# The eight modulation slots of the first norm in places of their own, and a ring of two that begins with the query weights

## The chip, the cores and the metric

The kernel runs on one core of one Trainium2 chip. The metric is the device time of one execution in microseconds (us); the time given for a kernel is the median of its runs. Lower is better. Each core has a matrix engine (TensorE, PE in the tables, with its weight loads as PEld), a vector engine (DVE), a scalar engine (ACT), a fourth compute engine (GpSimd, POOL), a sequencer that only issues transfers (SyncE, SP), and 16 DMA engines that carry all transfers, whichever engine issued them.

## The reference, cut to what matters

A two-layer transformer block (x has 512 tokens, a context 256 tokens, width 1024) is followed by a second block with convolution, a recurrence and 32 routed experts. What the change touches is the very start: the modulation vectors and the first norm.

```python
silu_c = jax.nn.silu(c)
silu_cc = jax.nn.silu(c_ctx)
for l in range(DEPTH):
    mod = silu_c @ w_mod[l] + b_mod[l]          # w_mod[l]: 1024 x 6144
    mod_c = silu_cc @ w_mod[l] + b_mod[l]
    sh1, sc1, g1, sh2, sc2, g2 = jnp.split(mod[:, None, :], 6, axis=-1)
    csh1, csc1, cg1, csh2, csc2, cg2 = jnp.split(mod_c, 6)
    h = modulate(rms_norm(x, norm1[l]), sh1, sc1)
    hc = modulate(rms_norm(ctx, norm1[l]), csh1, csc1)
    na_q, na_k, na_v, gq, gk, gv, ga, gb = jnp.split(h @ w_in[l], IN_SPLITS, axis=-1)
    ...
```

The first norm needs `sh1`, `sc1` and their context twins: the first 2048 columns of `w_mod[0]`, which is 8 slots of 256 columns.

## The kernel before, in words

Activations are kept transposed: X is 8 tiles of 128 features by 768 tokens (512 of x, 256 of the context), all of it resident in on-chip memory. All weights of the two layers pass as one stream of slots. A slot is 1024 rows by 256 columns in float32, 128 partitions by 8 KB, 1 MB. They land in `ring`, which has two places: slot n goes to place n % 2. The order of the stream is that of `layer_slots`: for the first layer `mod_head` (8), then `gq` (2, the query weights), `gkv` (1) and so on.

What sets the order around the change is each engine's own program, written out by hand with semaphores:

- **SP** issues every slot (`load`, L464, and `load_at`, L488). Slot n waits until slot n - 2 has been used: for a modulation slot, until TensorE has multiplied with it (`steps`), for any other until GpSimd has made its lower part (`lo_done`).
- **ACT** first issues 18 transfers: `vecs` and `consts` (L1018, L1019), then 8 tiles of x and 8 of the context in turn (L1021, L1022). Then it computes the silu of both condition vectors into `sc2` (L1025), and the squares of the 8 tiles of X (L1046). The first square waits until all 16 tiles of X have landed. Then it makes the upper parts of the two halves of the first query slot (`upper`, L1077) and the root of the mean square (L1050).
- **TensorE** multiplies `sc2` with each modulation slot (L581), waits until DVE has copied the result into `mrow` (L1656), and turns it (`mod_turn`, L570). After the eighth it enters `spread_sum(0)`: it waits for all squares and sums, sums over partitions (L591, L592) and spreads the inverse root (L598). The projections are the products of L553.
- **GpSimd** adds up the squares (`sum_squares`, L1428 and L1431), then makes the lower parts of the first query slot (`lower`, L1440).
- **DVE** copies the modulation rows (L1656), adds the bias (L1635), takes the reciprocal (L1592, L1595), and multiplies X by the scale and the inverse root (L1623).

A product of two float32 matrices is made of three products of upper and lower parts (L553), so a slot has to be split before it can be used. The modulation slots are used as they are (`DIRECT`).

Of the kernel before, what the change touches and what calls it, by code (L numbers as in the profile page):

```python
# [8 lines left out]
KD = D // P  # L9
# [11 lines left out]
RING = 2  # L21
SLOT = KD * 256
# [3 lines left out]

def layer_slots(l):

    first = [("mod_head", 8)] if l == 0 else []
    return first + [("gq", 2), ("gkv", 1), ("nak", 2), ("naq", 2), ("nav", 2),  # L30
                    ("mod_rest", 24 if l == 0 else 16),
                    ("merge", 16), ("w_o", 4), ("ffn_in0", KH), ("ffn_out0", 8), ("ffn_in1", KH), ("ffn_out1", 8)]

# [1 line left out]

WIDTHS = {"merge": (8, 4), "ffn_out0": FFQ, "ffn_out1": FFQ}

EVACUATION = {"mod_head": "-", "mod_rest": "-", "merge": "AAVVAAVV", "w_o": "V", "ffn_in0": "AV", "ffn_in1": "AV",
              "ffn_out0": "--VV", "ffn_out1": "--VV", "w_in2": "AVAVAVAVAAAAAAAA", "w_out2": "V"}

DIRECT = ("mod_head", "mod_rest")

SLOT0 = {}
CHUNKS = []
# [101 lines left out]
NR = NG4 + NE  # L146


def build(nc, stream, vecs, consts, xT, ctxT, bias, experts, router, router_b, lru_w, w_ple, pT, w_gate, out):
    fp32 = mybir.dt.float32  # L150
    f32r = mybir.dt.float32r
    ALU = mybir.AluOpType
# [5 lines left out]
    with es:  # L158
# [3 lines left out]
        def sem(name):  # L162
            return es.enter_context(nc.semaphore(name))
# [3 lines left out]
        def at(name, first, size, dtype=fp32):  # L167


            with ExitStack() as place:  # L170
                if first:
                    place.enter_context(nc.sbuf_tensor(f"below_{name}", [P, first], fp32))
                return place.enter_context(nc.sbuf_tensor(name, [P, size], dtype))

        B0 = 16384
        ring = at("ring", 0, RING * SLOT).rearrange("p (r n) -> p r n", n=SLOT)
        h_parts = at("h_parts", 4096, 2 * KD * T, f32r)
        B = at("first_block", B0, 26112)
        BR = at("half_slots", B0 + 22016, 4 * D, f32r)
        y_parts = at("y_parts", B0 + 9216, 2 * KD * T, f32r)  # L180
# [18 lines left out]
        sc2 = sb("sc2", [P, KD, 32])  # L199
# [25 lines left out]
        V = view(B, 9984, 6, 640)  # L225
# [20 lines left out]
        ps = [es.enter_context(nc.psum_tensor(f"ps{i}", [P, 1024], fp32)) for i in range(4)]  # L246
# [13 lines left out]

        loaded = [sem(f"slot{r}_loaded") for r in range(RING)]
        steps = sem("steps_done")
        evac = {"A": sem("scalar_evacuated"), "V": sem("vector_evacuated")}
        inputs = sem("inputs_loaded")
        x_loaded = sem("x_loaded")
# [161 lines left out]
        def updating_step(n, m):  # L427
# [2 lines left out]
                return 2 * SLOT0[n // 2, "w_o"] + m  # L430
            return 2 * SLOT0[n // 2 - 1, "ffn_out1"] + 4 * (m // 2) + 2 + m % 2

        def raw_half(s):

            n = s // 2
            w = ring[:, n % RING, 0:CHUNKS[n] * 256].rearrange("p (k n) -> p k n", n=256)
            return w[:, :, (s % 2) * P:(s % 2 + 1) * P]
# [14 lines left out]
        @block.sync  # L452
        def _(sp):
            def load(n, i=0):

                m = n - RING
                if m >= 0 and SPLIT[2 * m]:

                    sp.wait_ge(lo_done, 8 * i + splits(2 * m + 1))
                elif m >= 0:  # L460

                    sp.wait_ge(steps, 8 * i + (2 * m + 2))
                k = CHUNKS[n]
                sp.dma_start(ring[:, n % RING, 0:k * 256],  # L464
                             stream[ds(4 * i + n, 1), :, 0:k * 256].rearrange("a p n -> p (a n)"))\
                  .then_inc(loaded[n % RING], 16)

            def load_phase(n0, count):
                for n in range(n0, n0 + min(count, 4)):
                    load(n)  # L470
                rounds = count // 4 - 1
                if rounds > 0:

                    with sp.Fori(1, 1 + rounds) as i:
                        for n in range(n0, n0 + 4):
                            load_at(n, i)
                for n in range(n0 + 4 + 4 * max(rounds, 0), n0 + count):
                    load(n)

            def load_at(n, i):  # L480

                m = n + 4 - RING
                if SPLIT[2 * m]:
                    sp.wait_ge(lo_done, 8 * i + (splits(2 * m + 1) - 8))
                else:
                    sp.wait_ge(steps, 8 * i + (2 * m - 6))
                k = CHUNKS[n]
                sp.dma_start(ring[:, n % RING, 0:k * 256],  # L488
                             stream[ds(4 * i + n, 1), :, 0:k * 256].rearrange("a p n -> p (a n)"))\
                  .then_inc(loaded[n % RING], 16)  # L490

            for l in range(LAYERS):
                for name, count in layer_slots(l):
                    load_phase(SLOT0[l, name], count)
            load_phase(SLOT0[2, "w_in2"], 8)
            load_phase(SLOT0[2, "w_out2"], 4)

            sp.wait_ge(steps, 2 * N_STREAM)
            for q in range(12):
                sp.dma_start(MR[:, q, :], experts[0, q]).then_inc(m_load[q], 16)  # L500
            sp.dma_start(scr[:, 5120:7168], w_ple).then_inc(p_in, 16)
            sp.dma_start(scr[:, 7168:8192], pT).then_inc(p_in, 16)
            sp.wait_ge(r_ok, 1)
            total = sp.value_load(total_i[0:1, 0:1], min_val=PAIRS, max_val=PAIRS * (NL // CAP))
            with sp.Fori(1, total) as i:
                j = i % PAIRS
                for q in range(12):

                    sp.wait_ge(m_steps, 12 * i + (q // 2 * 2 - 10))
                    sp.dma_start(MR[:, q, :], experts[ds(j, 1), q].rearrange("a p n -> p (a n)")).then_inc(m_load[q], 16)  # L510

            sp.wait_ge(m_steps, 12 * total)
            for q in range(4):
                sp.dma_start(MR[:, q, :], w_gate[q]).then_inc(pg_in, 16)

            for k in range(KD):
                sp.wait_ge(x_upd, 17 + k)
                sp.dma_start(out[k * P:(k + 1) * P, :], X[:, k, 0:NL]).then_inc(xo, 16)
            sp.wait_ge(xo, 16 * KD)
# [3 lines left out]
        def _(pe):  # L523
# [38 lines left out]
            kept = []  # L562

            def mod_turn():
# [5 lines left out]
                    last = nc.tensor.matmul(ps[3][:, c:c + 2], mrow[:, half * P:(half + 1) * P], fold, start=True, stop=True)  # L570
                last.then_inc(mod_turned, 1)

            def mod_slot(n, tile, l, first=False):

                if not first:
                    mod_turn()
                wait_slot(n)
                w = ring[:, n % RING, :].rearrange("p (k n) -> p k n", n=256)
                for k in range(KD):
                    g = 32 * (k % 4)  # L580
                    last = nc.tensor.matmul(ps[3][g:g + 32, 512:768], sc2[:, k, :], w[:, k, :], start=k < 4, stop=k >= 4)  # L581
                last.then_inc(steps, 2)
                kept.append((tile, l))

            def spread_sum(n, nt):
# [14 lines left out]

            pe.wait_ge(inputs, 32)
            pe.wait_ge(silu_done, 1)
            for n in range(8):
                mod_slot(n, 2 * n, 0, n == 0)
            mod_turn()

            for l in range(LAYERS):
# [41 lines left out]
                nav = 2 * SLOT0[l, "nav"]  # L649
                for j in range(18):  # L650
                    s = s0 + j
# [179 lines left out]
            for j in range(16):  # L831
                s = s0 + j
# [15 lines left out]
            for j in range(8):  # L848
                t, g = j // 2, j % 2
# [11 lines left out]
            for t in range(4):  # L861
                last = nc.tensor.matmul(ps[2][:, 0:NL], onesm, CV[:, t, :], start=t == 0, stop=t == 3)
# [8 lines left out]
            for j in range(8):  # L871
                s = s0 + j
# [144 lines left out]
        def _(act):  # L1017
# [52 lines left out]
            def upper(s, per=0, i=0):  # L1070

                if not is_split(s):
                    return
                act.wait_ge(loaded[(s // 2) % RING], 4 * per * i + 16 * (s // 4 + 1))

                act.wait_ge(steps, per * i + (s - 1))
                act.activation(part(0, s), raw_half(s), ACT.Copy).then_inc(hi_done, 1)  # L1077

            act.wait_ge(small_ok, 1)
# [508 lines left out]
        def _(dve):  # L1588
# [62 lines left out]
            for l in range(LAYERS):  # L1651
                nc.vector.tensor_scalar(qg8[:, l:l + 1], vcol(f"q_gain{l}"), QSCALE, None, ALU.mult).then_inc(small_q, 1)

            for n in range(8):
                dve.wait_ge(steps, 2 * n + 2)
                nc.vector.tensor_copy(mrow[:, :], ps[3][:, 512:768]).then_inc(mod_kept, 1)  # L1656
            dve.wait_ge(mod_turned, 8)
            mod_add(0, 0, 16)
# [454 lines left out]
def slots(w):  # L2113

    k, n = w.shape
    return w.reshape(k // P, P, n // 256, 256).transpose(2, 1, 0, 3).reshape(n // 256, P, -1)


def lay_out(x):
# [4 lines left out]
    def put(l, name, blocks):  # L2124
        n = SLOT0[l, name]
        for b in blocks:
            z[n:n + b.shape[0], :, :b.shape[2]] = b
            n += b.shape[0]

    for l in range(LAYERS):  # L2130
        wm, w = x["w_mod"][l], x["w_in"][l]
        if l == 0:
            put(0, "mod_head", [slots(wm[:, :2048])])
            put(0, "mod_rest", [slots(wm[:, 2048:]), slots(x["w_mod"][1][:, :2048])])
        else:
            put(1, "mod_rest", [slots(wm[:, 2048:])])
# [56 lines left out]
    def by_rows(a):  # L2193

        return a.reshape(-1, P, a.shape[-1]).transpose(1, 0, 2).reshape(P, -1)

    return {"stream": z, "vecs": v, "consts": constants(), "xT": np.ascontiguousarray(x["x"][0].T[:, BLOCKS]),
            "ctxT": np.ascontiguousarray(x["ctx"][0].T), "bias": bias_tables(x["na_rpb"]), "experts": experts,
            "router": router, "router_b": router_b, "lru_w": np.concatenate([x["lru_w_r_2"], x["lru_w_i_2"]]),
            "w_ple": by_rows(x["w_ple_2"][0]), "pT": by_rows(x["p_2"][0, 0].T[:, BLOCKS]), "w_gate": slots(x["w_ple_gate_2"][0])}  # L2200
# [52 lines left out]
```

## Time and profile before

| what | us |
|---|---|
| median of 3 runs | 3204.75 |
| lowest and highest run | 3204.34, 3209.13 |
| the profiled execution, device time | 3203.88 |
| its span, first to last instruction | 3202.1 |
| PE busy | 2970.2 |
| DVE busy | 958.7 |
| ACT busy | 877.6 |
| POOL busy | 930.2 |

The times of the trace are counted from the first instruction of the span. Busy times are of instructions only; a PE that is busy need not run at its peak, since matmuls are pipelined. In the time slices of the page the matrix engine is busy 60% of the first slice of 80 us and 90% or more of most others. The mean granted TensorE clock is 0.965 of full speed.

### The profile page before, as it was taken

What the parts mean: (1) busy time and instruction counts of PE and PEld (TensorE: products, weight loads), DVE (VectorE), ACT (ScalarE), POOL (GpSimd) and SP (SyncE); (2) the same over time, 40 slices, a digit from 0 to 9 for tenths busy, and PEclk for the clock granted to TensorE, in tenths of its full rate; (3) what the DMA queues carried; (4) which work ended last, traced back from release to release, by engine and by line L of the source; (5) the groups of instructions that cost most, each with busy time, mean ns of one, the idle gap of its engine ahead of it and who ended that gap; (6) DMA issues with size and microseconds to landing.
All of it is one profiled execution on the core that took longest, in us unless ns stands there. A gap on an engine that the chain in (4) does not pass through costs nothing.

```text
span 3202.1 us, 42037 instructions
## 1 busy us (share of the span) xinstructions
PE 2970.2 (93%) x17158; PEld 2241.0 (70%) x17158; DVE 958.7 (30%) x1378; ACT 877.6 (27%) x1415; POOL 930.2 (29%) x707
## 2 busy tenths in 40 slices
PE   6999889998999999899889999998877899999998
PEld 4887678887888888687667778886745645454453
DVE  2505541022110211423531232121494322223224
ACT  3226441123221222325442232223333111111121
POOL 3323223333223223432224444445572000000011
PEclk9999999999999999899999999998988799999999
DMA  5124321111112111123222222322211688888840
GB/s 198 63 72 169 108 67 64 67 53 53 66 49 76 66 51 61 62 80 117 98 67 85 87 85 91 106 84 94 68 43 60 288 327 359 358 358 328 357 166 27
DMA packets 62184, 406.49 MB, mean 127 GB/s; under 512 B 7232, under 2 KB 8656, under 8 KB 18160
## 3 DMA queue, kind: packets, MB, share of 16 engines
q1 hardware_dynamic: 57600, 393.77, 33.0%
q0 software_dynamic: 1872, 6.72, 0.6%
q10 hardware_dynamic: 2592, 4.30, 0.4%
q8 instruction: 88, 1.44, 0.2%
q14 instruction: 32, 0.26, 0.0%
HBM read 402.66 MB, written 2.10 MB: 126 GB/s over the span
## 4 chain that ended last, share of the span: by engine, by line
PE 78%; issue 8%; DVE 7%; POOL 3%; ACT 2%; ACTq 0%; DMA 0%; POOLq 0%; DVEq 0%
PE ps L553 45%; PE ps L942 7%; PE ps L917 4%; PE ps L965 4%; PE ps L712 3%; POOL half_slots L1440 3%; PE ps L739 3%; PE ps L693 2%; DVE second_block L1912 2%; PE ps L1010 2%; PE ps L982 2%; PE ps L581 2%; DVE X L2085 1%; PE ps L570 1%; PE ps L598 1%
## 5 line engine op out<-in xcount | busy, mean ns | idle before, releaser
L553 PE MATMUL ps<-h_parts,half_slots 128*128 128x512 f32 (+1 forms) x6240 | 1233.1, 359 | 44.7 <-POOL half_slots L1440 14.5
L553 PEld LDWEIGHTS ps<-h_parts,half_slots 128*128 128x128 f32 x6240 | 1039.7, 191 | 239.7 <-issue 38.3
L1440 POOL TENSOR_TENSOR half_slots<-ring,half_slots 128x1024 fp32r<-128x1024 f32 (+3 forms) x292 | 631.4, 2163 | 961.2 <-ACT half_slots L1077 960.9
L1077 ACT ACTIVATE half_slots<-ring 128x1024 fp32r<-128x1024 f32 (+3 forms) x292 | 280.3, 961 | 1340.8 <-PE ps L553 1330.0
L553 PE MATMUL ps<-hidden_parts,half_slots 128*128 128x512 f32 (+1 forms) x1584 | 305.1, 355 | 0.0
L553 PEld LDWEIGHTS ps<-hidden_parts,half_slots 128*128 128x128 f32 x1584 | 261.0, 188 | 43.6
L553 PE MATMUL ps<-y_parts,half_slots 128*128 128x512 f32 (+1 forms) x1152 | 230.5, 361 | 9.9 <-DVE y_parts L1766 9.7
L553 PEld LDWEIGHTS ps<-y_parts,half_slots 128*128 128x128 f32 x1152 | 193.9, 192 | 44.5 <-issue 11.7
L942 PE MATMUL ps<-second_block,scratch 128*64 128x512 f32 x1024 | 223.3, 593 | 1.2 <-DVE scratch L2056 0.6
L1428 POOL COPY second_block<-second_block 128x512 f32<-128x512 f32 x4 | 2.5, 628 | 700.6 <-ACT second_block L1046 700.6
L942 PEld LDWEIGHTS ps<-second_block,scratch 128*64 128x64 f32 x1024 | 86.5, 137 | 130.6 <-issue 130.6
L1819 DVE TENSOR_TENSOR first_block<-ps,first_block 128x768 f32<-128x768 f32 (+1 forms) x44 | 36.3, 824 | 434.0 <-PE ps L553 434.0
L1187 ACT ACTIVATE first_block<-ps,small 128x512 f32<-128x512 f32 (+2 forms) x160 | 115.7, 728 | 141.3 <-DVE small L1731 81.7
L1800 DVE SCALAR_TENSOR_TENSOR X<-ps,mod,X 128x512 f32<-128x512 f32 x72 | 45.4, 659 | 357.6 <-PE ps L553 357.6
L712 PE MATMUL ps<-cst,first_block 128*128 128x128 f32 x704 | 106.9, 282 | 32.6 <-ACT first_block L1175 32.6
L917 PEld LDWEIGHTS ps<-scratch,second_block 128*128 128x128 f32 x816 | 103.5, 194 | 30.6 <-issue 26.0
L965 PE MATMUL ps<-second_block,scratch 128*64 128x512 f32 x512 | 113.4, 595 | 11.8 <-ACT scratch L1389 11.8
L917 PE MATMUL ps<-scratch,second_block 128*128 128x128 f32 x816 | 118.3, 282 | 4.5 <-DVE scratch L2060 4.5
L712 PEld LDWEIGHTS ps<-cst,first_block 128*128 128x128 f32 x704 | 74.3, 141 | 64.6 <-ACT first_block L1187 39.5
L1711 DVE COPY first_block<-ps 128x512 f32<-128x512 f32 x112 | 77.3, 690 | 134.8 <-PE ps L712 134.4
L1783 DVE TENSOR_TENSOR first_block<-ps,first_block 128x768 f32<-128x768 f32 (+3 forms) x32 | 26.4, 824 | 295.0 <-PE ps L553 295.0
L1826 DVE TENSOR_TENSOR hidden_parts<-first_block,hidden_parts 128x768 f32 (+3 forms) x44 | 97.3, 2211 | 47.6 <-ACT hidden_parts L1274 47.6
(265 smaller groups left out, 2907.3 us busy)
## 6 DMA issues: line engine op xcount, KB each, us to landing
second_block<-experts SPq DMA_DIRECT2D x192, 1024.0 KB, 8.0
ring<-stream SPq DMA_DIRECT2D x146, 1024.0 KB, 4.9
ring<-stream SPq DMA_DIRECT2D x16, 768.0 KB, 4.2
ring<-stream SPq DMA_DIRECT2D x16, 640.0 KB, 3.9
ring<-stream SPq DMA_DIRECT2D x16, 512.0 KB, 3.6
first_block<-bias POOLq DMA_DIRECT2D x16, 384.0 KB, 4.4
second_block<-w_gate SPq DMA_DIRECT2D x4, 1024.0 KB, 8.0
X<-xT ACTq DMA_DIRECT2D x8, 256.0 KB, 9.2
```

Source lines behind the costliest of these rows:

```text
L553: last = nc.tensor.matmul(ps[s % 2][:, a:b], part(x, s)[:, k, :], parts[y][:, tile + k, a:b], start=start and k == 0 and n == 0, stop=stop ...
L581: last = nc.tensor.matmul(ps[3][g:g + 32, 512:768], sc2[:, k, :], w[:, k, :], start=k < 4, stop=k >= 4)
L712: last = nc.tensor.transpose(ps[2][:, at:at + P], rows[:, (c % nch) * P:(c % nch + 1) * P], ident)
L739: nc.tensor.matmul(ps[3][half * HD:(half + 1) * HD, at:at + P], vals, p_turned(g)[:, (half * nch + c) * P:(half * nch + c + 1) * P], start ...
L917: last = nc.tensor.matmul(ps[0][:, k * P:(k + 1) * P], htok(c, k), SEL[:, c * P:(c + 1) * P], start=c == 0, stop=c == 3)
L942: last = nc.tensor.matmul(ps[1][CAP * x:CAP * x + CAP, 512 * w13:512 * w13 + 512], XG[:, 4 * kk + k, x * CAP:(x + 1) * CAP], w, start=kk = ...
L965: last = nc.tensor.matmul(ps[2][CAP * x:CAP * x + CAP, 512 * n:512 * n + 512], GT[:, 2 * kk + k, x * CAP:(x + 1) * CAP], w, start=kk == 0 ...
L1077: act.activation(part(0, s), raw_half(s), ACT.Copy).then_inc(hi_done, 1)
L1187: act.activation(p_rows(u)[:, 0:width(pairs[i])], ps[half][:, score_cols(g)], ACT.Exp, bias=small[:, 0, u % 8:u % 8 + 1], scale=-1.0 if ki ...
L1440: nc.gpsimd.tensor_tensor(part(1, s), raw_half(s), part(0, s).bitcast(fp32), ALU.subtract)\
L1711: nc.vector.tensor_copy(p_turned(g0 + i)[:, 512 * n:512 * n + 512], ps[2][:, 512 * (j % 2):512 * (j % 2) + 512]).then_inc(s_pt["V"], 1)
L1826: nc.vector.tensor_tensor(dst, g, hi.bitcast(fp32), ALU.subtract).then_inc(gs_lo, 1)
```

## The change

The eight slots of `mod_head` leave the stream and become an input of their own, `mod_head`. Each has its own place in memory, six right behind the ring in what later holds `h_parts`, two in the space of the first block, and a semaphore of its own. SP issues all eight at its start, without a wait. Behind them it issues the first two slots of `gq`, which now are slots 0 and 1 of the ring and have no wait either. TensorE waits for slot n's own semaphore; DVE waits for a new semaphore, `head_steps`. ACT's upper parts of the very first slot no longer wait for `steps`. The stream of the ring is 8 slots shorter, an even number, so every later slot keeps its place.

```diff
-    first = [("mod_head", 8)] if l == 0 else []
-    return first + [("gq", 2), ("gkv", 1), ("nak", 2), ("naq", 2), ("nav", 2),
+    return [("gq", 2), ("gkv", 1), ("nak", 2), ("naq", 2), ("nav", 2),
...
+        head_low, head_high = at("mod_head_low", 4096, 6 * SLOT), at("mod_head_high", B0 + 9216, 2 * SLOT)
...
+        head_in = [sem(f"mod_head{n}_loaded") for n in range(HEAD_SLOTS)]
+        head_steps = sem("mod_head_done")
...
+        def head_slot(n):
+
+            place, at = (head_low, n) if n < 6 else (head_high, n - 6)
+            return place[:, at * SLOT:(at + 1) * SLOT]
...
+            for n in range(HEAD_SLOTS):
+                sp.dma_start(head_slot(n), mod_head[n]).then_inc(head_in[n], 16)
             for l in range(LAYERS):
                 for name, count in layer_slots(l):
                     load_phase(SLOT0[l, name], count)
...
-            for n in range(8):
-                mod_slot(n, 2 * n, 0, n == 0)
+            for n in range(HEAD_SLOTS):
+                if n:
+                    mod_turn()
+                pe.wait_ge(head_in[n], 16)
+                mod_rows(head_slot(n)).then_inc(head_steps, 1)
+                kept.append((2 * n, 0))
             mod_turn()
...
-                act.wait_ge(steps, per * i + (s - 1))
+                if s >= 2:
+                    act.wait_ge(steps, per * i + (s - 1))
...
-            for n in range(8):
-                dve.wait_ge(steps, 2 * n + 2)
+            for n in range(HEAD_SLOTS):
+                dve.wait_ge(head_steps, n + 1)
```

`mod_rows` is the loop of eight matmuls that stood in `mod_slot`, now used by both.

On SP, at the start of the program, before the change (L464 and L488 are the ring's loads, 128x2048 is one slot of 1 MB):

```order
L452 UNCONDITIONAL_BRANCH [waits barrier_Pool_Activation_PE_DVE_SP_release]
L464 DMA ring<-stream 128x2048 x2
L464 DMA ring<-stream 128x2048 [waits steps_done] x2
L474 UNCONDITIONAL_BRANCH
L488 DMA ring<-stream 128x2048 [waits steps_done] x4
L474 REGISTER_ALU
L474 COMPARE_AND_BRANCH
L464 DMA ring<-stream 128x2048 [waits steps_done] x2
L464 DMA ring<-stream 128x2048 [waits both_parts_ready] x9
```

And now (L501 are the eight loads of their own, L472 the ring's):

```order
L460 UNCONDITIONAL_BRANCH [waits barrier_Pool_Activation_PE_DVE_SP_release]
L501 DMA mod_head_low<-mod_head 128x2048 x6
L501 DMA mod_head_high<-mod_head 128x2048 x2
L472 DMA ring<-stream 128x2048 x2
L472 DMA ring<-stream 128x2048 [waits both_parts_ready] x9
```

Two loads without a wait became ten; the first that waits is the third of the ring, for the split of its predecessor.

On TensorE, the end of the head and the start of the norm before (L581 multiplies with a slot, L570 turns its row, L591 begins the sum over partitions):

```order
L581 MATMUL ps<-ring,sc 32x256 [waits slot1_loaded]
L581 MATMUL ps<-ring,sc 32x256 x7
L570 MATMUL ps<-cst,mod_rows 128x2 [waits mod_rows_kept]
L570 MATMUL ps<-cst,mod_rows 128x2
L591 MATMUL ps<-cst,first_block 128x1 [waits squared,squares_summed]
```

And now, at the same place:

```order
L588 MATMUL ps<-mod_head_high,sc 32x256 [waits mod_head7_loaded]
L588 MATMUL ps<-mod_head_high,sc 32x256 x7
L580 MATMUL ps<-cst,mod_rows 128x2 [waits mod_rows_kept]
L580 MATMUL ps<-cst,mod_rows 128x2
L605 MATMUL ps<-cst,first_block 128x1 [waits squared,squares_summed]
```

TensorE's instructions stand in the same order; only what each slot's first matmul waits for is another semaphore. The wait for the squares and their sums stays where it was.

## Rows read from the trace of the kernel before

**Rows 1.** The page: busy time, and the chain that ended last, by engine.

```profile
PE 2970.2 (93%) x17158; PEld 2241.0 (70%) x17158; DVE 958.7 (30%) x1378; ACT 877.6 (27%) x1415; POOL 930.2 (29%) x707
PE 78%; issue 8%; DVE 7%; POOL 3%; ACT 2%; ACTq 0%; DMA 0%; POOLq 0%; DVEq 0%
```

**Rows 2.** Chain in order of time, 0:110 us: start, duration, what.

```profile
15.99 6.11 DMA ring<-stream
...
30.98 5.26 DMA ring<-stream
...
43.20 0.43 PE ps L591 x2
```

**Rows 3.** Timeline: start, duration, engine, line, count, idle before and releaser.

```profile
12.39 1.28 ACT L1025 ACT_TABLE_LOAD   x1 [12.39 <-issue]
...
14.00 1.94 PE L581 MATMUL ps<-ring,sc 128*32 128x256 f32 x16 [14.00 <-ACT sc L1025]
...
25.57 1.93 PE L581 MATMUL ps<-ring,sc 128*32 128x256 f32 x16
...
28.99 1.93 PE L581 MATMUL ps<-ring,sc 128*32 128x256 f32 x16
...
39.71 1.93 PE L581 MATMUL ps<-ring,sc 128*32 128x256 f32 x16
...
43.07 0.56 PE L591 MATMUL ps<-cst,first_block 128*128 128x1 f32 x2
```

**Rows 4.** Waits, 0:60 us, PE: who waited for whom, us in total, times, longest.

```profile
PE ps L581 <- DMA ring<-stream: 1.5, 2, 1.2
```

**Rows 5.** Timeline: the squares and their sum.

```profile
19.70 1.57 ACT L1046 ACTIVATE first_block<-X 128x768 f32<-128x768 f32 x2 [5.79 <-DMA X<-ctxT]
...
21.58 11.58 POOL L1431 TENSOR_TENSOR first_block<-first_block 128x768 f32<-128x768 f32 x6 [0.15 <-POOL first_block L1428]
```

**Rows 6.** DMA view of 3:6 us, then of 6:10 us: queue, packets, MB, share.

```profile
q1 hardware_dynamic: 136, 0.99, 78.4%
q10 hardware_dynamic: 142, 0.25, 21.8%
...
q1 hardware_dynamic: 112, 0.91, 53.6%
q10 hardware_dynamic: 108, 0.81, 48.0%
```

**Rows 7.** Stretches: window, length, PE, PEld, DVE, ACT, POOL busy, PEclk, DMA share, GB/s.

```profile
3.00:6.00 3.00, 0.00 (x0) 0.00 (x0) 0.00 (x0) 0.00 (x0) 0.00 (x0) 1.00 1.00 415
6.00:10.00 4.00, 0.00 (x0) 0.00 (x0) 0.00 (x0) 0.00 (x0) 0.00 (x0) 1.00 1.02 430
11.00:17.00 6.00, 2.46 (x19) 1.21 (x19) 0.64 (x3) 1.50 (x2) 0.00 (x0) 1.00 1.07 377
2472.00:2506.00 34.00, 24.15 (x117) 22.18 (x118) 14.00 (x40) 5.52 (x10) 0.00 (x0) 0.60 1.01 412
```

**Rows 8.** The page, DMA issues: count, KB each, median us to landing.

```profile
X<-xT ACTq DMA_DIRECT2D x8, 256.0 KB, 9.2
X<-ctxT ACTq DMA_DIRECT2D x8, 128.0 KB, 8.9
cst<-consts ACTq DMA_DIRECT2D x1, 947.0 KB, 10.2
vec<-vecs ACTq DMA_DIRECT2D x1, 182.0 KB, 5.8
```

**Rows 9.** Timeline: transfers issued by ACT at the start, by SP before the experts.

```profile
5.47 1.79 ACTq L1022 DMA_DIRECT2D X<-ctxT  x1
...
11.85 0.45 ACTq L1022 DMA_DIRECT2D X<-ctxT  x1
...
2471.18 7.38 SPq L500 DMA_DIRECT2D second_block<-experts  x12
2478.60 2.11 SPq L501 DMA_DIRECT2D scratch<-w_ple  x1
```

**Rows 10.** Timeline: the first query slot's parts, two spreads of equal shape, first product.

```profile
42.99 2.00 ACT L1077 ACTIVATE half_slots<-ring 128x1024 fp32r<-128x1024 f32 x2 [10.84 <-DMA ring<-stream]
...
44.12 4.66 POOL L1440 TENSOR_TENSOR half_slots<-ring,half_slots 128x1024 fp32r<-128x1024 f32 x2 [10.96 <-ACT half_slots L1077]
...
49.90 2.93 PE L598 MATMUL ps<-first_block,cst 128*128 128x512 f32 x4 [1.57 <-DVE first_block L1595]
...
56.49 2.26 PE L553 MATMUL ps<-h_parts,half_slots 128*128 128x512 f32 x6 [3.66 <-DVE h_parts L1612]
...
78.98 1.45 PE L619 MATMUL ps<-first_block,cst 128*128 128x512 f32 x4
```

More of the change, by code:

```diff
@@ L36 @@
 WIDTHS = {"merge": (8, 4), "ffn_out0": FFQ, "ffn_out1": FFQ}
-EVACUATION = {"mod_head": "-", "mod_rest": "-", "merge": "AAVVAAVV", "w_o": "V", "ffn_in0": "AV", "ffn_in1": "AV",
+EVACUATION = {"mod_rest": "-", "merge": "AAVVAAVV", "w_o": "V", "ffn_in0": "AV", "ffn_in1": "AV",
               "ffn_out0": "--VV", "ffn_out1": "--VV", "w_in2": "AVAVAVAVAAAAAAAA", "w_out2": "V"}
-DIRECT = ("mod_head", "mod_rest")
+DIRECT = ("mod_rest",)
+HEAD_SLOTS = 8
 SLOT0 = {}
@@ L146, with build @@
 NR = NG4 + NE
-def build(nc, stream, vecs, consts, xT, ctxT, bias, experts, router, router_b, lru_w, w_ple, pT, w_gate, out):
+def build(nc, stream, mod_head, vecs, consts, xT, ctxT, bias, experts, router, router_b, lru_w, w_ple, pT, w_gate, out):
     fp32 = mybir.dt.float32
@@ L571, in mod_turn, with mod_rows @@
                 last.then_inc(mod_turned, 1)
+            def mod_rows(w):
+                w = w.rearrange("p (k n) -> p k n", n=256)
+                for k in range(KD):
+                    g = 32 * (k % 4)
+                    last = nc.tensor.matmul(ps[3][g:g + 32, 512:768], sc2[:, k, :], w[:, k, :], start=k < 4, stop=k >= 4)
+                return last
             def mod_slot(n, tile, l, first=False):
@@ L577, in mod_slot @@
                 wait_slot(n)
[L578 to L582, printed above, removed]
+                mod_rows(ring[:, n % RING, :]).then_inc(steps, 2)
                 kept.append((tile, l))
@@ L2132, in lay_out @@
         if l == 0:
-            put(0, "mod_head", [slots(wm[:, :2048])])
             put(0, "mod_rest", [slots(wm[:, 2048:]), slots(x["w_mod"][1][:, :2048])])
@@ L2195, in by_rows @@
         return a.reshape(-1, P, a.shape[-1]).transpose(1, 0, 2).reshape(P, -1)
-    return {"stream": z, "vecs": v, "consts": constants(), "xT": np.ascontiguousarray(x["x"][0].T[:, BLOCKS]),
+    return {"stream": z, "mod_head": slots(x["w_mod"][0][:, :2048]), "vecs": v, "consts": constants(), "xT": np.ascontiguousarray(x["x"][0].T[:, BLOCKS]),
             "ctxT": np.ascontiguousarray(x["ctx"][0].T), "bias": bias_tables(x["na_rpb"]), "experts": experts,
```

## The prediction

> **What bounds the kernel now.** I read the page first: TensorE is busy 93% of the span and has 78% of the chain that ended last, while DMA has 0% of it after rounding [rows 1]. So bandwidth matters only where TensorE stands still, and the change touches nothing but the first 45 us. The second view is the chain in order of time for that stretch [rows 2]. It passes through the ring's loads twice (6.11 and 5.26 us), and this looks like what the change is after. Then it enters the sum over partitions at 43.20. The third view, the timeline, corrects that picture [rows 3]: ACT's silu starts at 12.39, after its 18 issues, and TensorE begins the first slot at 14.00. Undisturbed, slot follows slot in 28.99 - 25.57 = 3.42 us: matmuls, DVE's copy, the turn. Eight of these from 14.00 would end at 41.36, and L591 in fact starts at 43.07, so loads cost the head about 1.7 us. The waits say the same: 1.5 us of TensorE for the ring in two waits [rows 4].
>
> There is a second path into L591. It waits for the sums of squares, too. ACT begins to square at 19.70, released by the last tile of X; the sum ends on POOL at 21.58 + 11.58 = 33.16 [rows 5]. That is 13.46 us from the landing of X to the last sum, and 43.07 - 33.16 = 9.9 us of slack. X can land as late as 29.6 before it costs anything.
>
> **The change part by part.**
>
> *Eight loads without the ring's waits.* At most this takes away the 1.5 to 1.7 us that TensorE waits for slots: L591 could start at 14.00 + 27.36 = 41.36 instead of 43.07. That is the whole gain on offer. It is 0.05% of 3204.75.
>
> *What now queues beside X.* Before, SP had two slots in flight while ACT's transfers ran, and nothing more until TensorE was done with the first. Its slots and ACT's `vecs` and `consts` ended together, and from 11 us X had the engines to itself: in 11:17 they moved 377 GB/s, with no SP traffic [rows 7]. Now SP has ten slots queued from the first microseconds: the eight, and the two of `gq`, which do not wait either. So 8 more slots, 8 x 1024 KB = 8.39 MB, stand beside X.
>
> How the engines share decides all. The trace shows both queues with work in 3:10: in 3:6, 136 packets of q1 (SP's) and 142 of q10 (ACT's); in 6:10, 112 and 108 [rows 6]. They take turns packet by packet, although in 3:6 the bytes stood at 0.99 to 0.25 MB. One packet is one partition's row: 8 KB for a slot, 2 KB for a tile of x (256 KB over 128 rows), 1 KB for one of the context [rows 8]. X has 16 transfers x 128 = 2048 packets, the eight slots have 8 x 128 = 1024. If they alternate, all 1024 packets of the slots have passed when X is half through. So all 8.39 MB move before X has landed. Both queues together moved 415 and 430 GB/s [rows 7]; I take 420. 8.39 MB / 420 GB/s = 20.0 us. X lands at 19.7 + 20.0 = 39.7.
>
> A check by the total: 10 slots, 182, 947, 8 x 256 and 8 x 128 KB [rows 8] are 14441 KB = 14.79 MB. At 420 GB/s that is 35.2 us, and the flow sets in at about 3 us: 38 to 39. The stretch 2472:2506, where 14 transfers of SP were in flight, kept 412 GB/s over 34 us [rows 7], so the rate holds for that long. Bounds: the fastest mixed row, 430 GB/s, gives 19.5 us more; the slowest, 377, gives 22.3. If mixing small packets with large ones hides some of the small packets' cost, the total's 38 stands as the lower end.
>
> On the HBM limit the Trainium skill speaks otherwise: its page "DMA: Bandwidth & Descriptors", section Specifications, gives about 358 GB/s for one core. By it the 8.39 MB would take an estimated 23.4 us and the result would be some 3.4 us later than mine. This case's trace disagrees, with 412 to 430 GB/s over up to 34 us.
>
> *The slots under this sharing.* Each of the slots 2 to 7 takes its own 1.05 MB and some 0.2 MB of X, 1.25 MB / 420 = 3.0 us. They land every 3.0 us from about 11 on, faster than the 3.42 us in which TensorE uses them. TensorE no longer waits for them; its head ends at about 41.4, and there it now meets the squares.
>
> *The second path.* 39.7 + 13.46 = 53.2 for the last sum. ACT's and POOL's instructions there are unchanged. L591 then starts at 53.2 instead of 43.07: **+10.1 us**.
>
> *What is late next.* Everything behind L591 moves with it. The upper parts of the first query slot come after the squares on ACT (2.00 us), the lower ones after the sum on POOL (4.66 us) [rows 10]. Before they ended at 48.78, 7.7 us ahead of the first product at 56.49. Now they end at about 53.2 + 4.9 = 58.1, and the first product stands at about 66.6: still 8.5 us ahead. The earlier landing of `gq` and the wait on `steps` that ACT drops are worth nothing, then. The ring's third slot waits for these lower parts and moves with them, as it did before.
>
> *TensorE's clock.* The head stands still for some 12 us more. The spread at 49.90 takes 2.93 us for the same four instructions that take 1.45 at 78.98 [rows 10], at a granted clock of 1.00 in the neighbouring rows; so before the products TensorE already ran at the lower of its two levels, 1.2 GHz, and there is nothing to lose by the idle time. The rise comes behind L553's start, which only moves. I put it at 0.
>
> *Sum.* -1.7 that the head could give is swallowed by the later bound; +10.1 net. Profiled execution: 3203.88 + 10.1 = 3214.0. The median of the runs is 0.87 above that execution: 3214.9. I forecast 3214.5. The bounds of the X landing, 38 to 42, make +8.4 to +12.4: 3212 to 3217.
>
> **The rivals.**
>
> *A: X is not held up.* If the engines shared by bytes, or if X's packets were fetched ahead of the slots', X would land by 24 (4.30 MB of ACT's against as much of SP's, 8.6 / 420 = 20.5 us, from 3) or not later at all. Below 29.6 the squares stay hidden, and the head ends 1.7 us earlier: 3203.0. For it: alternation between slots and X itself is not in the trace, only between slots and `vecs`, `consts`. Against it: bytes of 0.99 to 0.25 with packets of 136 to 142 [rows 6]. For this outcome the Trainium skill's page "DMA: Bandwidth & Descriptors", section Rules for kernel authors, says to issue a transfer early and wait late; here the early ones share engines with what is needed sooner. Landings between 29.6 and 36 give 0 to +6, in between. That it does not do what it says, since the engines were nearly full already (415 and 430 GB/s), also ends here: no more than 1.5 us can come of it.
>
> *B: ACT's issues are held up, and with them the silu.* It comes after all 18 issues. SP's 13th large transfer before the experts took 2.11 us to issue, where twelve took 7.38 together [rows 9]: a queue that is full makes the issuer wait. ACT's own issue at 5.47 took 1.79 us, but the last at 11.85 only 0.45; since `consts` took 10.2 us to land and tiles about 9 [rows 8], some 14 of its 18 were in flight then. If it held only 10 beside SP's load, the 18th would wait for the eighth landing: `vecs`, `consts` by 11.4 and six tiles at 3.0 us each, 29.4. TensorE's head would begin at about 31 and end 27.4 later at 58.4: +15.3, 3219.6. It decides only where the queue holds fewer than 12; with 12, the head ends at 52.4, just inside the squares' 53.2.
>
> *C: the same as my forecast, but slower transfer.* At 377 GB/s 3217. It is in the range.
>
> **How the numbers follow.** Forecast (X late) 0.78, A 0.13 (with its in-between landings), B 0.07, other 0.02. The range 3209 to 3220 holds the forecast with 3 us of doubt below 3212, and B; it leaves out A. A measurement of this kernel can tell about 0.2%, 6.4 us, from no change. The forecast is +0.30%. Slower by more: the forecast nearly whole, 0.76, with B 0.06: 0.82. Within: A and the forecast's lower edge, 0.16. Faster by more than 0.2%: no case has more than 1.8 us to give, 0.02.
>
> **What would show it.** The first square starts near 39.7 and is released by X; the first L591 is released by POOL's sum, near 53.2; TensorE has no wait for a modulation slot past the first, and its last turn ends near 41.4; the DMA view of 12:34 shows as many packets of q1 as of q10; the first product starts near 66.6. I am wrong if the first square starts before 30, if q10 gets through more packets than q1 in 12:34, or if the silu starts much after 12.4.

## The result, and the profile after

The changed kernel takes 3221.48 us (median of 5 runs, 3216.44 to 3222.43) against 3204.75 before (median of 5, 3199.30 to 3209.13): ratio 1.0051, 95% interval 1.0038 to 1.0064. It is slower, by 16.7 us in the medians. I had forecast slower, by about 10 us, and a range that ends at 3220; the time lies above it. Two executions in the comparisons further down, one of the kernel before (5163 us) and one of e3 (3810 us), ran at a much lower granted clock (0.645 and 0.744) and stand in no ratio.

The page of the changed kernel shows next to nothing of it. Busy time on every engine is within 2.1 us of [rows 1], the span is 17.6 us longer (3219.7 against 3202.1):

```profile
PE 2968.1 (92%) x17158; PEld 2239.0 (70%) x17158; DVE 959.0 (30%) x1378; ACT 877.5 (27%) x1415; POOL 930.1 (29%) x707
PE 78%; issue 8%; DVE 7%; POOL 3%; ACT 2%; ACTq 1%; POOLq 0%; DVEq 0%
```

Work has not grown, so something starts later. The timeline of the first 75 us (start, duration, engine, line, count; idle before and releaser) says what. These rows answer [rows 3, 5, 9]:

```profile
5.15 0.47 ACTq L1039 DMA_DIRECT2D X<-xT  x1
5.65 1.62 ACTq L1040 DMA_DIRECT2D X<-ctxT  x1
7.30 3.05 ACTq L1039 DMA_DIRECT2D X<-xT  x1
10.39 2.53 ACTq L1040 DMA_DIRECT2D X<-ctxT  x1
...
23.57 0.46 ACTq L1039 DMA_DIRECT2D X<-xT  x1
24.06 7.64 ACTq L1040 DMA_DIRECT2D X<-ctxT  x1
31.79 1.28 ACT L1043 ACT_TABLE_LOAD   x1 [31.79 <-issue]
...
33.40 1.94 PE L588 MATMUL ps<-mod_head_low,sc 128*32 128x256 f32 x16 [33.40 <-ACT sc L1043]
...
39.47 1.57 ACT L1064 ACTIVATE first_block<-X 128x768 f32<-128x768 f32 x2 [6.17 <-DMA X<-ctxT]
...
41.35 11.59 POOL L1450 TENSOR_TENSOR first_block<-first_block 128x768 f32<-128x768 f32 x6 [0.15 <-POOL first_block L1447]
...
60.71 0.57 PE L605 MATMUL ps<-cst,first_block 128*128 128x1 f32 x2
...
74.13 2.26 PE L563 MATMUL ps<-h_parts,half_slots 128*128 128x512 f32 x6 [3.66 <-DVE h_parts L1631]
```

From the tenth of its 18 issues on, ACT is held up: the tenth takes 1.62 us, the next six, which would take half a microsecond with room in the queue, take 2.5 to 3.1 each, the seventeenth goes at once (0.46), and the last takes 7.64. SP had issued the last of its ten slots by 6.97, so ACT does not wait for SP's issues but for transfers to drain. So the silu comes at 31.8 instead of 12.4, and TensorE, which waits for nothing else by then, starts the head at 33.40 instead of 14.00. Its eight slots go by at 3.42 us each without one wait for a load, and the sum over partitions starts at 60.71 instead of 43.07: +17.64 us. From there on both traces run in step: from this sum to the first product it takes 13.42 us in both (43.07 to 56.49; 60.71 to 74.13), and SP's first transfer of the experts is issued 17.54 us later (2471.18; 2488.72). That the spans differ by 17.6 us, too, is in part luck. Executions drift apart behind the start by themselves: e3, below, starts its sum within 0.04 us of before and has a span that is 2.9 us longer (3205.0); e4 starts it 3.17 us late and has one that is 2.3 us shorter (3199.8).

X itself arrives at 39.47 instead of 19.70, and its last sum on POOL ends at 52.94. This is the second loss, side by side with the first and hidden behind it.

### The profile page after: what moved, and what is told of

It reads as the page before. It is cut to its first block, busy times and chain, and to the rows that moved or that the text cites. A ratio compares the mean times of both kernels' runs of the same rounds, so it can differ in the third digit from the quotient of the medians.

```text
span 3219.7 us, 42032 instructions
## 1 busy us (share of the span) xinstructions
PE 2968.1 (92%) x17158; PEld 2239.0 (70%) x17158; DVE 959.0 (30%) x1378; ACT 877.5 (27%) x1415; POOL 930.1 (29%) x707
## 3 DMA queue, kind: packets, MB, share of 16 engines
q10 hardware_dynamic: 2592, 4.30, 0.4%
## 4 chain that ended last, share of the span: by engine, by line
PE 78%; issue 8%; DVE 7%; POOL 3%; ACT 2%; ACTq 1%; POOLq 0%; DVEq 0%
PE ps L563 45%; PE ps L960 7%; PE ps L935 4%; PE ps L983 4%; PE ps L730 3%; POOL half_slots L1459 3%; PE ps L757 3%; PE ps L711 2%; DVE second_block L1931 2%; PE ps L588 2%; PE ps L1028 2%; PE ps L1000 2%; DVE X L2104 1%; PE ps L580 1%; PE ps L612 1%
## 5 line engine op out<-in xcount | busy, mean ns | idle before, releaser
L983 PE MATMUL ps<-second_block,scratch 128*64 128x512 f32 x512 | 113.4, 595 | 11.8 <-ACT scratch L1408 11.8
L1802 DVE TENSOR_TENSOR first_block<-ps,first_block 128x768 f32<-128x768 f32 (+3 forms) x32 | 26.4, 825 | 295.2 <-PE ps L563 295.2
```

The lines of the kernel that those rows point to most:

```text
L983: last = nc.tensor.matmul(ps[2][CAP * x:CAP * x + CAP, 512 * n:512 * n + 512], GT[:, 2 * kk + k, x * CAP:(x + 1) * CAP], w, start=kk == 0 ...
```

## The experiments

In all of them four times are read from the timeline: when TensorE starts the head, when ACT starts the first square (X is in), when POOL's last sum of squares ends, and when the sum over partitions starts. The last is the measure. Single runs of the unchanged kernel spread from 3198 to 3209 us on the chips used, so of a few microseconds the start of the trace tells more than the medians do. Each ratio is to the kernel before on the same chip.

| run | head starts | first square | last sum on POOL | sum over partitions | shift | ratio, 95% interval |
|---|---|---|---|---|---|---|
| before | 14.00 | 19.70 | 33.16 | 43.07 | | |
| the change | 33.40 | 39.47 | 52.94 | 60.71 | +17.64 | 1.0051 (1.0038 to 1.0064) |
| e1, silu early | 11.58 | 40.79 | 54.21 | 54.26 | +11.19 | 1.0034 (1.0022 to 1.0046) |
| e2, e1 and gq late | 11.65 | 35.57 | 48.99 | 49.05 | +5.98 | 1.0022 (1.0011 to 1.0033) |
| e3, two in flight | 13.97 | 19.64 | 33.12 | 43.11 | +0.04 | 0.9999 (0.9988 to 1.0011) |
| e4, four in flight | 18.92 | 24.74 | 38.20 | 46.24 | +3.17 | 1.0008 (0.9996 to 1.0020) |
| e6, X in pairs | 28.36 | 39.37 | 52.84 | 55.67 | +12.60 | 1.0034 (1.0021 to 1.0047) |
| e8, X in 8 KB rows | 11.77 | 26.43 | 39.92 | 39.97 | -3.10 | 0.9990 (0.9981 to 0.9999) |
| e7, before, silu early | 11.60 | 24.63 | 38.10 | 41.97 | -1.10 | 0.9991 (0.9982 to 1.0000) |
| e10, before, 8 KB rows | 11.58 | 19.39 | 32.87 | 42.08 | -0.99 | 0.9999 (0.9990 to 1.0008) |
| e5, interleaved | 6.65 | 12.12 | 35.04 | 38.20 | -4.87 | 0.9995 (0.9985 to 1.0004) |
| e9, interleaved, 8 KB | 6.67 | 13.57 | 30.62 | 39.79 | -3.28 | 0.9991 (0.9982 to 1.0001) |

### e1: the silu ahead of ACT's last ten issues

```diff
             for k in range(KD):
+                if k == 3:
+                    act.wait_ge(inputs, 32)
+                    act.wait_ge(sc_zero, 1)
+                    act.activation(sc2[:, :, 0:2], ...)
                 act.dma_start(X[:, k, 0:NL], ...)
```

> The change, but ACT computes the silu after its first eight issues (vecs, consts and the first three tiles of x and of the context) and issues the rest of X behind it. Theory (two losses side by side: X lands behind all ten queued slots, and ACT's issues are held up, which made the silu late; the later of the two sets the start of the sum over partitions, L591 before): the silu starts near 12, TensorE's head ends near 41.4, X still lands near 39.5, the last sum on POOL near 52.9, so the sum over partitions starts near 53 instead of 60.7: 7.7 us less than the change, ratio to before 1.003 (3215). Rival 1 (the late silu is the only loss): the sum over partitions starts at 41.4, 3203. Rival 2 (ACT stands still for another reason than its full queue): the silu stays near 32, 3221.

```profile
11.58 1.94 PE L588 MATMUL ps<-mod_head_low,sc 128*32 128x256 f32 x16 [11.58 <-ACT sc L1042]
...
40.79 1.57 ACT L1065 ACTIVATE first_block<-X 128x768 f32<-128x768 f32 x2 [29.30 <-DMA X<-ctxT]
...
54.26 0.58 PE L605 MATMUL ps<-cst,first_block 128*128 128x1 f32 x2 [15.20 <-POOL first_block L1451]
```

The timeline of e1: TensorE now starts at 11.58, is through with the head at about 39 and then stands still for 15.20 us, released by POOL's sum. The sum over partitions moves from 60.71 to 54.26, where the theory had 53; X came 1.3 us later than in the change. Both rivals fall: the silu was one loss, and 11.2 us remain without it. That remainder is what I had forecast (+10.1).

### e2: e1, with the query weights held back

```diff
             for n in range(HEAD_SLOTS):
                 sp.dma_start(head_slot(n), mod_head[n]).then_inc(head_in[n], 16)
+            sp.wait_ge(head_steps, HEAD_SLOTS - 1)
```

> As the run with the early silu, and SP holds the two loads of gq back until TensorE has done seven modulation slots, as before the change. Theory (X lands behind every slot that stands in SP's queue, 2.5 us each): X lands near 34.4, the last sum near 47.9, 5 us less than with gq in the queue: 3210, ratio 1.0015. Rival (only the total of bytes in the first 40 us counts, or only the eight loads of their own do): no difference from the run with the early silu, 3215.

```profile
35.57 1.58 ACT L1066 ACTIVATE first_block<-X 128x768 f32<-128x768 f32 x2 [24.03 <-DMA X<-ctxT]
...
49.05 0.59 PE L606 MATMUL ps<-cst,first_block 128*128 128x1 f32 x2 [9.94 <-POOL first_block L1452]
```

Two slots fewer in the queue bring X 5.22 us earlier, 2.6 us a slot, and the sum over partitions by the same. In e1 nobody read `gq` before 53.1 (ACT's first upper part), and its place in the queue cost 5 us. The forecast 34.4 for X missed by 1.2 us.

### e3 and e4: two and four slots in flight

```diff
             for n in range(HEAD_SLOTS):
+                if n >= 2:                      # e4: n >= 4, n - 3
+                    sp.wait_ge(head_steps, n - 1)
                 sp.dma_start(head_slot(n), mod_head[n]).then_inc(head_in[n], 16)
+            sp.wait_ge(head_steps, HEAD_SLOTS - 1)
```

> The change, but SP issues slot n of the eight only when TensorE has done slot n - 2, and gq after the seventh, as the ring did: the places of their own stay, 'all at once' goes. Theory (all of the loss comes from what is in the queue, none from the places): X lands near 19.6, silu at 12.4, the sum over partitions starts near 43.1, ratio 1.000 (3204.8). Rival (the places or the second load site cost something): some us over before.

> The change, but four slots in flight at most: slot n is issued when TensorE has done slot n - 4, gq after the seventh. Theory: X lands 2.5 us later for each slot that gets ahead of it, two at once and one or two more that are issued while X is on its way, so near 25 to 30; ACT's issues are held up only while SP's queue is full, the silu starts by 12.4 to 16; the sum over partitions starts between 41.4 and 45: 3203 to 3207, ratio 0.9995 to 1.0006. Rival (the losses do not grow with the number of slots queued but come as soon as more than two are): X near 39, 3215 or more.

e3 gives the time of before to 0.04 us in the timeline: the places of their own cost and give nothing, all of the loss is in what is queued. e4 lies between. Its timeline shows both losses at a lower dose:

```profile
7.38 3.06 ACTq L1042 DMA_DIRECT2D X<-xT  x1
10.47 2.52 ACTq L1043 DMA_DIRECT2D X<-ctxT  x1
...
13.02 1.31 ACTq L1042 DMA_DIRECT2D X<-xT  x1
14.36 0.46 ACTq L1043 DMA_DIRECT2D X<-ctxT  x1
...
18.92 1.93 PE L591 MATMUL ps<-mod_head_low,sc 128*32 128x256 f32 x16 [18.92 <-ACT sc L1046]
...
24.74 1.58 ACT L1067 ACTIVATE first_block<-X 128x768 f32<-128x768 f32 x2 [5.92 <-DMA X<-ctxT]
```

ACT is held up until 14.33, when 481 of the 576 packets of SP's four slots have moved, and then goes on at 0.5 to 0.7 us an issue. X is in 5.10 us later than with two in flight (24.74 against 19.64): two slots more, some 2.5 us each. My price for the head was too low: the silu comes at 17.31, where I had put it at 16 at the latest, and the sum starts at 46.24, where I had put 45 at the latest. The head starts 4.9 us late, and 3.2 of that arrive, since TensorE no longer waits for slots.

### e6: X in 8 transfers instead of 16, the same rows

```diff
-            for k in range(KD):
-                act.dma_start(X[:, k, 0:NL], xT[k * P:(k + 1) * P, :])...
+            for k in range(0, KD, 2):
+                act.dma_start(X[:, k:k + 2, 0:NL], xT[k * P:(k + 2) * P, :].rearrange("(a p) n -> p a n", p=P))...
```

> The change, but X in 8 transfers of two tiles each instead of 16, the same rows: ACT has 10 issues instead of 18. Question: is what ACT's queue holds counted in transfers or in rows? Transfers (about ten, as the issue times of the change and of the run with the early silu suggest): ACT is never held up, silu near 11.4, X still lands near 39.4, the sum over partitions starts near 53: 3215. Rows (about ninety on each DMA engine): ACT is held up from its seventh issue on, the silu comes at 25 to 32, the head ends after 53 to 61: up to 3221.

```profile
4.14 3.25 ACTq L1039 DMA_DIRECT2D X<-xT  x1
...
7.43 5.95 ACTq L1040 DMA_DIRECT2D X<-ctxT  x1
13.40 0.49 ACTq L1039 DMA_DIRECT2D X<-xT  x1
13.93 12.73 ACTq L1040 DMA_DIRECT2D X<-ctxT  x1
...
39.37 1.57 ACT L1064 ACTIVATE first_block<-X 128x768 f32<-128x768 f32 x2 [11.11 <-DMA X<-ctxT]
```

ACT has 10 issues, and is held up all the same, from the seventh on; its silu starts at 26.75. So no fixed number of transfers fills the queue: six were let through here, nine in the change. Their bytes do not fill it either, since e8 (next) issues 4.30 MB in five transfers without a hold. That leaves the rows: at the first held issue ACT had handed over 80 for each of the 16 DMA engines here (two transfers of 128 rows, four of 256), and 72 in the change.

One fixed limit does not come out of it, though. The page counts 144 packets for a transfer of 128 rows, 16 of them small, and the DMA view from 0 to the start of the held issue says how many had moved. Per engine, 83 packets were still to move here (86 less 3), and 72 in the change (81 less 9). Yet in the change 87 at 23.57 held nothing up, and in the kernel before 110 at 11.85 did not.

X arrives as in the change, 39.37 against 39.47, though its last issue ended 5 us earlier (26.66 against 31.70) and it came in half as many transfers: the same rows, the same share.

### e8: X in rows as long as the slots'

x and the context are laid out in memory as they stand on the chip, and come in 3 transfers of 128 rows of 8 KB; SP's ten slots stay as in the change.

```diff
-                act.dma_start(X[:, k, 0:NL], xT[k * P:(k + 1) * P, :]).then_inc(x_loaded, 16)
-                act.dma_start(X[:, k, NL:T], ctxT[k * P:(k + 1) * P, :]).then_inc(x_loaded, 16)
+            rows = X[:, :, :].rearrange("p k t -> p (k t)")
+            for j in range(3):
+                act.dma_start(rows[:, SLOT * j:SLOT * (j + 1)], xall[:, SLOT * j:SLOT * (j + 1)]).then_inc(x_loaded, 16)
```

> The change with all ten slots in SP's queue, but x and the context laid out in memory as they stand on the chip, so that X comes in 3 transfers with rows of 8 KB, 384 rows instead of 2048, the same bytes. Theory (the engines take turns row by row): only 384 rows of the slots get ahead of X, so X lands near 26.4 instead of 39.4; ACT has 5 issues, silu near 11.3; slots land every 5.2 us until X is in, then every 2.6; head and squares both end near 40: 3201.5, ratio 0.999. Rival (X lands last because its transfers are issued last, or because SP goes ahead): X near 37 to 39 again, the sum over partitions at 51 or later, 3213 or more.

The DMA view of 12:26 (queue, packets, MB, share), first of the change, then of e8:

```profile
q1 hardware_dynamic: 674, 4.87, 83.8%
q10 hardware_dynamic: 674, 0.94, 18.4%
```

```profile
q1 hardware_dynamic: 433, 3.15, 54.0%
q10 hardware_dynamic: 386, 2.77, 47.3%
```

In the change 674 packets stand against 674, and ACT's queue gets 0.94 MB beside 4.87. In the window that I had named, 12:34, it is 1050 against 1052. In e8 the numbers are again near each other (ACT's is 11% lower), and now so are the bytes. X is in at 26.43 instead of 39.47, and I had written 26.4. The timeline of e8:

```profile
26.43 1.58 ACT L1064 ACTIVATE first_block<-X 128x768 f32<-128x768 f32 x2 [14.76 <-DMA X<-xall]
...
39.97 0.58 PE L605 MATMUL ps<-cst,first_block 128*128 128x1 f32 x2
```

Nothing was issued in another order here, and SP's queue held as much as in the change. X's rows are longer and fewer, and its transfers are 3 instead of 16; e6 shows that fewer transfers and an earlier last issue alone do not bring X in sooner. So the queues share by the number of rows, whatever a row's length. Whether they change after each row or after a few, these counts do not tell. With the silu on time and X in 13 us earlier, the kernel is faster than before: -3.10 us in the timeline, 0.9990 in the runs. Of the 3.10, not all comes from loading all at once; e10 divides it.

### e7 and e10: the kernel before, with the same two cures

e7 is the edit of e1, made to the kernel before; e10 is the edit of e8, made to it.

> The kernel before, with nothing but the silu moved ahead of ACT's last ten issues. Theory (the head is bound by its start, not by its loads): TensorE begins at 11.6 instead of 14.0, slots 2 and 3 are issued earlier and delay X to 22 to 25, which its slack covers; the sum over partitions starts at 41 instead of 43.1: 3202.7, ratio 0.9993. Rival (the loads bind): TensorE starts earlier and waits for slot 2 instead, 43, 3204.8.

> The kernel before, with its ring of two for all slots, and X in 3 transfers of 8 KB rows on ACT's queue. Question: once X no longer suffers, what are the eight places of their own worth? Theory: ACT has 5 issues, so the silu comes at 11.3; X lands near 21, the ring's slots come two at a time, TensorE waits for slots 2 and 3, and the sum over partitions starts near 41.5, against 40.0 of the change with 8 KB rows: the places are worth 1.5 us, ratio 0.9995. Rival (places worth nothing, the gain is all of the rows): 40.0 here, too; rival (worth more than that): 43.

They ask what the ring's waits for loads cost once TensorE starts early. In the first fence e7, in the second e10:

```profile
19.86 1.93 PE L581 MATMUL ps<-ring,sc 128*32 128x256 f32 x16 [1.36 <-DMA ring<-stream]
...
24.43 1.94 PE L581 MATMUL ps<-ring,sc 128*32 128x256 f32 x16 [1.07 <-DMA ring<-stream]
...
41.97 0.56 PE L591 MATMUL ps<-cst,first_block 128*128 128x1 f32 x2
```

```profile
21.07 1.93 PE L581 MATMUL ps<-ring,sc 128*32 128x256 f32 x16 [2.58 <-DMA ring<-stream]
...
42.08 0.57 PE L591 MATMUL ps<-cst,first_block 128*128 128x1 f32 x2
```

In e7 the head starts 2.40 us earlier and gives back 1.3 of it, mostly in waits for slots (2.7 us instead of 1.5). The sum starts at 41.97, between the 41 that I expected and the 43 of the rival. e10 gets to 42.08 (expected 41.5) and waits 2.58 us for its third slot. Against e10, e8 is 2.11 us ahead (39.97 to 42.08); that is what the eight places and the loads without a wait are worth in the timeline once X has long rows, and two thirds of e8's 3.10. The other 0.99 comes with ACT's shorter list of issues and the long rows, in e10. In the runs e10 cannot be told from before (0.9999), and e8 and e10 ran on different chips.

### e5 and e9: versions in the order of need

e5 keeps the eight places, but SP issues everything in one queue: slots 0 and 1, tiles 0 and 1 of X, then slot n and tile n in turn, `gq` last. ACT issues `vecs` and `consts` only and computes the silu when `vecs` is in; each square waits for its own tile. TensorE no longer waits for `consts` before the first slot, only before the first turn. The cuts leave out the semaphores that this needs. e9 is the same with X in 3 transfers of 8 KB rows, behind slots 1, 2 and 4.

```diff
             for n in range(HEAD_SLOTS):
                 sp.dma_start(head_slot(n), mod_head[n]).then_inc(head_in[n], 16)
+                if n == 1:
+                    x_tile(0)
+                if n:
+                    x_tile(n)
...
-            act.wait_ge(inputs, 32)
+            act.wait_ge(vec_in, 16)
...
-                        act.wait_ge(x_loaded, 32 * (m + 1) if m == KD - 1 else 256)
+                        act.wait_ge(x_in[m], 32)
```

> A version made from the findings. The eight places of their own stay, but SP issues everything in the order of need in one queue: slots 0 and 1, tiles 0 and 1 of X, then slot n and tile n in turn, gq last. ACT issues only vecs and consts and computes the silu as soon as vecs has landed; each square waits for its own tile alone. Theory: silu near 7, the first slot's product near 7, the first turn when consts has landed (11.3), then 3.42 us a slot; slot and tile together take 3.5 us of transfer, so TensorE hardly waits and the sum over partitions starts near 36.8 instead of 43.1, squares done before it: 3204.75 - 6.3 = 3198.5, ratio 0.998. Rival (the first transfers are slowed by the small rows or by SP's issues, or the squares fall behind): 40 or later, 3202 or more.

> The interleaved version with X in three transfers of 8 KB rows (behind slots 1, 2 and 4) instead of 16: the same order of need, X cheaper on the DMA engines. In the interleaved version TensorE waited 1.6 us for a slot and the sum over partitions started at 38.2. Theory: vecs, consts, 8 slots and X are 12.7 MB, 33.3 us at 420 GB/s with the start; the last slot lands near 33.5 and the sum over partitions starts near 37: 6 us under before, ratio 0.998. Rival (the order costs as much as the rows give): 38 or later, ratio 0.9985 to 0.9995.

Waits of TensorE in 0:45 (who for whom, us in total, times, longest), e5 and then e9:

```profile
PE ps L601 <- ACT sc L1054: 6.7, 1, 6.7
PE ps L593 <- DMA cst<-consts: 2.7, 1, 2.7
PE ps L601 <- DMA mod_head_high<-mod_head: 1.6, 1, 1.6
```

```profile
PE ps L598 <- DMA mod_head_low<-mod_head: 3.5, 3, 1.7
```

e5 has the earliest sum over partitions of all, 38.20, which is 4.87 us ahead of before but 1.4 behind the 36.8 that I expected. Its runs (0.9995) do not show this gain beyond their interval. The trace says where most of it goes in the profiled execution: SP's first transfer of the experts is issued 4.63 us ahead of before (2466.55 against 2471.18), the transfer of the result only 1.33 us (3193.49 against 3194.82). In the profiles of all the other kernels here that stretch takes 723.6 to 723.9 us, in e5 726.9; TensorE waits 14.8 us instead of 11.8 for ACT's copies into `scratch` in it. Why is open. e9 was meant to improve on e5 and did not, 39.79: there its rival held. TensorE waits three times for a slot, 3.5 us in all. A block of X is as long as a slot, an estimated 2.5 us at 420 GB/s, so each pushes the slots behind it back by that; that this makes the three waits is argued, not tested.

## Why the prediction was wrong

**What bounds the kernel, and what the edit could give.** Right. TensorE has no wait for a modulation slot left, and e3 shows that the places alone change nothing. No run takes away the ring's waits alone; the nearest, e8 against e10, gives 2.11 us with a head that starts some 2.3 us earlier than in before, so 1.5 to 1.7 us was the right size.

**How the engines share.** Right, and now shown in the mix that [rows 6] could not show: 674 packets against 674 in 12:26, and e8 as the counter-test. A packet is not quite a row, though I wrote so: the page counts 2592 for ACT's 18 transfers, 144 each, 128 rows and 16 small ones. Both queues have them, so the sum is not touched. X was to be in at 39.7; ACT's first square starts at 39.47. My 420 GB/s stood for a rate of 414 in the change:

```profile
12.00:34.00 22.00, 0.60 (x8) 0.43 (x12) 0.00 (x0) 1.50 (x2) 0.00 (x0) 1.00 1.02 414
```

This is the row of the changed kernel for 12:34, with the columns of [rows 7]. The Trainium skill ("DMA: Bandwidth & Descriptors", Specifications) states about 358 GB/s for one core, which it works out as half of a stack's 716 GB/s. This kernel runs on one core alone, and 414 GB/s over 22 us exceed that figure; for such a kernel the measurement decides.

**The second path.** Right: 39.47 + 13.47 = 52.94 for the last sum, forecast 53.2. What ran beside it on ACT and POOL did not change.

**The head at 41.4.** Wrong, and this is the step that failed. The forecast had the silu unchanged at 12.4. It was late by 19.4 us, and the head, not the squares, set the start of the norm: 60.71 instead of 53.2. This was rival B, to which I had given 0.07. Its mechanism was named and its price was close (+15.3 for a queue that holds 10; +17.64 measured), but I had put it aside by a number from the wrong state: "some 14 of its 18 were in flight" was read at 11.85, when SP's two slots had gone and X had the engines to itself. The rows that bore on the question were ACT's tenth issue at 5.47 (1.79 us) and SP's thirteenth (2.11 us) in [rows 9], both from a time in which long rows kept the queues moving slowly: with slots beside it ACT's queue moved 674 packets in 14 us (the change, 12:26), with X alone 1658 in 6 us (before, 11:17). With ten slots in SP's queue that state lasted past 31 us. In before, issues are held up twice and end at 8.53; with four slots (e4) this ends at 14.33, with ten at 31.70.

**What came late behind it.** Right: no other term. The first product stands 13.42 us behind the start of the sum in both kernels, and the query weights' parts were ready long before it, at 57.60 (forecast 58.1). It came at 74.13 instead of the forecast 66.6 only because the sum did. The spread after the sum took 2.93 us as in [rows 10], at the lower of TensorE's two levels, 1.2 GHz, with the granted clock at 1.00, and the first six products took 2.26 us in both traces: the longer idle time cost no clock.

**The range.** It took in B at 3219.6 and ended 1.5 us under the measured median. The +17.64 of the trace on top of the profiled 3203.88 is 3221.5; that this meets the median to a tenth is luck, since the interval of the ratio leaves 12 to 21 us. The part of B's price that was missing, 2.3 us, is the 18th issue: I let it go at 29.4, after the eighth landing, and it ended at 31.70. By then 1300 packets of ACT's queue had moved (DMA view of 0:31.7), which is nine transfers of 144.

**Rival A and its rule.** X was held up, so A fell. The rule of the Trainium skill behind it ("DMA: Bandwidth & Descriptors", Rules for kernel authors: issue early, wait late) gives 2.11 us in e8 against e10, where the early loads leave what is needed sooner enough of the engines, and costs 17.6 us in the change, where they do not.

**What stays open.** How much a queue holds. Issues were held with 72 (the change) and 83 (e6) packets an engine still to move, and went through with 87 (the change) and 110 (before). That rows count, and not transfers or bytes, rests on e6 and e8 alone, and what sets the limit no run here settles.

## What to carry to other kernels

Before loads are moved ahead, list what else is on its way then and when it is needed: a load that waits for nothing still takes its share, row for row, beside one that is waited for. Short rows lose most beside long ones, so give what is urgent longer rows (e8), or put both into one queue in the order of need (e5, whose lead shows in the trace of the start and not in the runs). And look at what stands behind an engine's issues in its own program: an issue is an instruction that can be held up by a full queue, and a compute step that the whole kernel waits for does not belong behind eighteen of them.

## What the runs showed of the hardware

- Two queues with work share the DMA engines by the number of rows, not by bytes: 674 packets against 674 in 14 us at 8 KB against 2 and 1 KB (the change), and 433 against 386 at 8 KB each (e8).
- An issue on ACT took 0.45 us with room in its queue; held up beside ten slots of SP, 2.5 to 7.6 us for 128 rows (the change) and up to 12.73 us for 256 (e6). The engine does nothing else meanwhile: the silu behind it came 19.4 us late.
- One more slot of 1 MB in SP's queue delayed X by some 2.6 us (5.10 us for two in e4 against e3, 5.22 for two in e1 against e2).
- One core read 414 GB/s over 22 us (the change, 12:34) and 423 over 14 us (e8, 12:26).
